# A hybrid decoder layer on 8 cores: mixer phase first, channel mixer in 1024-token tiles, probabilities as the stationary operand

## The chip, the cores and the metric

The kernel runs on the 8 cores of one Trainium2 chip. Each core computes one of the 8 sequences of the batch, with no traffic between cores. The metric is the device time in microseconds of the slowest core; lower is better. TensorE is PE in the profile, with its weight loads on a row of their own (PEld); VectorE is DVE, ScalarE is ACT, GpSimd is POOL, SyncE is SP. Every DMA is issued from the queue of an engine: in this kernel weights from POOL's, all else from SP's.

## What is computed

Per sequence of 2048 tokens and 2048 channels, one layer (the reference, cut):

```python
a = rms_norm(h, norm1_g)
q, k, v, u, sv, gates = split(a @ w_in)      # 1024 each, gates 4096
# A: 8 heads, each with two 64-wide q/k pairs and one 128-wide v
q = apply_rope(rms_norm(q)); k = apply_rope(rms_norm(k))
p = softmax(causal(q k^T / 8))               # two maps per head
o = (p[0] - lam * p[1]) @ v
o = rms_norm(o, subln_g) * 0.8
att_branch = o @ w_att_out
# B: gelu(u) * (causal 128x128 mix per group of layer_norm(gelu(sv)) + b)
sgu_branch = spatial_gating(gelu(u), gelu(sv)) @ w_sgu_out
g_att, g_sgu = split(sigmoid(gates + b_gate))
h = h + (g_att * att_branch + g_sgu * sgu_branch) @ w_out
# channel mixer
c = rms_norm(h, norm2_g)
up = causal_dwconv(c @ w_up, width 3)        # 2 * 5632
h = h + (gelu(up[:5632]) * up[5632:]) @ w_down
```

## The kernel before, in words

The program is written as one list of operations; `Sched.add` records each with the buffers that it reads and writes, and each engine runs its own operations in the order of that list, waiting on semaphores for earlier writers and readers. A read of a PSUM bank counts as a write of it. There is no scheduler: the order of the text is the order of every engine.

The outer loop takes four tiles of 512 tokens, and each tile runs the whole layer. `norm_to_T` (L331 to L350) squares and sums each of four 128-token chunks on ACT, gets the reciprocal root by Ln and Exp on ACT, scales on DVE (L339), transposes 16 blocks on PE (L346) and copies them out on DVE (L350). Then come q and k (L414, with two helper matmuls per head, L378 and L380), v (L432), u (L453) and sv (L469), v and sv in matmuls of 256 columns.

Attention runs head by head over blocks of 128 keys. Per block: two score matmuls with the keys stationary (L588, L591; 512 query columns, fewer on the diagonal), two Exp on ACT (L598, L600), a mask on the diagonal (L604), and one block later four matmuls, V or a matrix of ones stationary and the probabilities moving (L616, L619), into banks 4 to 7. The ones give the softmax sums. Then the spatial mix (L645, L650, L653), the gates and the two branch projections (L668, with the tanh of L680 and the merge of L689 to L695), and the output projection (L702, added to x in `hh`, which stays in SBUF). A second `norm_to_T` feeds the channel mixer: three groups of up to 16 hidden chunks, each up projection with convolution (L724 to L755) followed by its down projection (L768), added to `hh` (L782). The last group stores the result to `out` (L786, L779). The x loads of the next tile (L365) write `hh`, so they wait for those stores.

Weights pass through a ring of four slots of 1 MB (bf16; the source is fp32 in HBM, and the DMA of POOL's queue converts). A slot is reloaded when its last matmul has been issued (`wrel`, L262). The whole set of weights is read once per tile, four times in all.

## Time and profile before

| | |
|---|---|
| median of 3 runs | 4181.89 us (4176.98 to 4624.0) |
| profiled execution | 4176.65 us, its slowest core's span 4175.1 us |
| spans of the 8 cores | 4168.3 to 4175.1 us |
| PE busy, PEld, DVE, ACT, POOL | 90%, 46%, 42%, 30%, 7% of the span |
| DMA, POOL's queue | 494.96 MB written, 69.0% of the 16 DMA engines |
| DMA, SP's queue | 37.39 MB, 2.9% |

A matmul's end is modelled, so neighbours overlap in the busy figures; the pace of a stretch is read from starts. A DMA's bytes are those written; a weight of 1 MB in bf16 was 2 MB in HBM.

### The profile page before, as it was taken

Reading aid. Unit: us, or ns where it says so; the run is one execution under the profiler, and the core shown is the slowest. Engines: PE = TensorE matmul, PEld = TensorE weight load, DVE = VectorE, ACT = ScalarE, POOL = GpSimd, SP = SyncE. Lnnn points to the kernel's source line nnn. Section 1 sums busy time; section 2 is a strip of 40 time slices with the busy share of each in tenths; the row PEclk is TensorE's granted clock in tenths of the full one; section 3 lists DMA queues with packets and bytes.
Section 4 is the critical chain, followed back from the end, with each engine's and each line's share of the span. In section 5 each row is a group of like instructions: output and inputs, shape, how many; then the busy total and the mean of one; then the engine's idle time right before and its main releaser. Section 6 shows DMA issues by size and latency. Waiting matters only on the chain.

```text
span 4175.1 us, 56541 instructions; the slowest of 8 cores (4168.3 to 4175.1 us)
## 1 busy us (share of the span) xinstructions
PE 3774.7 (90%) x19565; PEld 1932.4 (46%) x19880; DVE 1735.9 (42%) x3544; ACT 1255.4 (30%) x2297; POOL 271.6 (7%) x516
## 2 busy tenths in 40 slices
PE   5969989995988989999598898999959989989999
PEld 2634644442553464444254346444425534554444
DVE  4251264642524137455342412645524122245545
ACT  3361031211465113112137611212214683121211
POOL 0001000000000100000000010000000000100000
PEclk9979999998999999999799999999979999999999
DMA  7809979989642878898772188789887305968887
GB/s 152 140 14 152 161 116 153 153 153 188 112 81 45 153 136 142 152 159 144 167 142 41 31 152 152 124 153 157 147 171 132 61 1 101 154 123 157 148 155 162
DMA packets 87398, 535.99 MB, mean 128 GB/s; under 512 B 9680, under 2 KB 9936, under 8 KB 29776
## 3 DMA queue, kind: packets, MB, share of 16 engines
q0 software_dynamic: 73728, 494.96, 69.0%
q1 hardware_dynamic: 13392, 37.39, 2.9%
q8 instruction: 166, 2.72, 0.3%
q14 instruction: 112, 0.92, 0.1%
HBM read 1010.46 MB, written 16.78 MB: 246 GB/s over the span
## 4 chain that ended last, share of the span: by engine, by line
PE 87%; DMA 5%; ACT 3%; DVE 3%; issue 2%; DVEq 0%; ACTq 0%; SPq 0%; POOLq 0%
PE ps L724 29%; PE ps L668 16%; PE ps L768 13%; PE ps L414 5%; PE ps L702 5%; PE ps L616 3%; PE ps L469 3%; PE ps L432 3%; PE ps L453 3%; PE ps L619 3%; DMA out<-sb_hh 3%; DMA sb_hh<-x 2%; PE ps L346 1%; PE ps L588 1%; PE ps L591 1%
## 5 line engine op out<-in xcount | busy, mean ns | idle before, releaser
L724 PE MATMUL ps<-sb_ar,sb_wr 128*128 128x512 bf16 x5516 | 1214.0, 380 | 6.8 <-issue 0.7
L724 PEld LDWEIGHTS ps<-sb_ar,sb_wr 128*128 128x128 bf16 x5632 | 552.0, 98 | 666.6 <-issue 5.4
L668 PE MATMUL ps<-sb_ar,sb_wr 128*128 128x512 bf16 x3008 | 670.3, 383 | 29.8 <-DVE sb_ar L653 17.4
L733 ACT ACTIVATE sb_tf<-ps,sb_pp 128x512 f32<-128x512 f32 x352 | 273.7, 778 | 1333.6 <-PE ps L724 1333.6
L768 PE MATMUL ps<-sb_wr,sb_ar 128*128 128x512 bf16 x2760 | 607.4, 379 | 6.5 <-DMA sb_wr<-w_down 3.5
L668 PEld LDWEIGHTS ps<-sb_ar,sb_wr 128*128 128x128 bf16 x3072 | 302.5, 99 | 396.5 <-issue 42.0
L768 PEld LDWEIGHTS ps<-sb_wr,sb_ar 128*128 128x128 bf16 x2816 | 275.2, 98 | 336.7 <-issue 5.4
L736 DVE SCALAR_TENSOR_TENSOR sb_tf<-ps,sb_pp,sb_tf 128x511 f32<-128x511 f32 x352 | 263.8, 749 | 253.9 <-ACT sb_tf L733 253.9
L782 DVE TENSOR_TENSOR sb_hh<-ps,sb_hh 128x512 f32<-128x512 f32 x176 | 121.7, 692 | 404.5 <-PE ps L768 404.5
L616 PE MATMUL ps<-sb_tb,sb_vv 128*128 128x512 bf16 (+3 forms) x627 | 220.2, 357 | 71.0 <-ACT sb_tb L598 25.7
L739 DVE SCALAR_TENSOR_TENSOR sb_tf<-ps,sb_pp,sb_tf 128x510 f32<-128x510 f32 x352 | 263.3, 748 | 38.8 <-DVE sb_tf L736 2.8
L346 PE MATMUL ps<-sb_cm,sb_ar 128*128 128x128 bf16 x512 | 59.7, 309 | 221.1 <-DVE sb_ar L339 221.1
L680 ACT ACTIVATE sb_tf<-ps,sb_hb 128x512 f32<-128x512 f32 x128 | 88.0, 687 | 517.1 <-PE ps L668 478.3
L414 PE MATMUL ps<-sb_ar,sb_wr 128*128 128x512 bf16 x1004 | 232.3, 384 | 1.7 <-DVE sb_ar L350 0.4
L619 PE MATMUL ps<-sb_tb,sb_cm 128*128 128x512 bf16 (+3 forms) x628 | 220.9, 357 | 12.1 <-ACT sb_tf L534 7.9
L702 PE MATMUL ps<-sb_wr,sb_ar 128*128 128x256 bf16 x2048 | 225.0, 273 | 1.9 <-DVE sb_ar L695 1.9
L689 DVE SCALAR_TENSOR_TENSOR sb_tf<-sb_tf,ps 128x512 f32<-128x512 f32 x64 | 43.7, 684 | 417.9 <-PE ps L668 417.9
L702 PEld LDWEIGHTS ps<-sb_wr,sb_ar 128*128 128x128 bf16 x2048 | 200.1, 98 | 27.0 <-issue 2.9
L331 ACT ACTIVATE sb_ar<-sb_hh 128x2048 bf16<-128x2048 f32 x32 | 60.8, 1899 | 481.9 <-PE ps L702 249.6
L262 POOL DMA_DIRECT2D sb_wr<-w_in x144 | 76.4, 531 | 1687.6 <-PE ps L564 567.7
L598 ACT ACTIVATE sb_tb<-ps 128x512 bf16<-128x512 f32 (+1 forms) x320 | 171.0, 534 | 44.4 <-PE ps L588 31.7
L262 POOL DMA_DIRECT2D sb_wr<-w_up x176 | 93.3, 530 | 1207.6 <-PE ps L724 892.0
(117 smaller groups left out, 3212.6 us busy)
## 6 DMA issues: line engine op xcount, KB each, us to landing
sb_wr<-w_up POOLq DMA_DIRECT2D x176, 1024.0 KB, 10.4
sb_wr<-w_in POOLq DMA_DIRECT2D x144, 1024.0 KB, 9.0
sb_wr<-w_down POOLq DMA_DIRECT2D x80, 1024.0 KB, 10.8
sb_wr<-w_out POOLq DMA_DIRECT2D x32, 1024.0 KB, 13.3
sb_hh<-x SPq DMA_DIRECT2D x16, 1024.0 KB, 12.7
sb_wr<-w_att_out POOLq DMA_DIRECT2D x32, 512.0 KB, 9.5
sb_wr<-w_sgu_out POOLq DMA_DIRECT2D x32, 512.0 KB, 8.6
out<-sb_hh SPq DMA_DIRECT2D x48, 256.0 KB, 26.7
```

The lines of the kernel that those rows point to most:

```text
L262: S.add("pool", lambda e, dst=dst, src=src: e.dma_start(out=dst, in_=src), writes=[("w", slot)], dma_key=("w", slot))
L414: S.add("pe", lambda e, bz=bz, kc=kc, wv=wv, half=half: e.matmul(ps[:, bz, :], lhsT=wv[:, kc, half * 128:(half + 1) * 128], rhs=ar[:, kc, ...
L598: S.add("act", lambda e, sb0=sb0, p0=p0, c0=c0: e.activation(out=tb[:, p0, c0:512], in_=ps[:, sb0, c0:512], func=AF.Exp), reads=[PS(sb0)], ...
L616: S.add("pe", lambda e, bo=bo, pq=pq, vsl=vsl: e.matmul(ps[:, bo, c0:512], lhsT=vsl, rhs=tb[:, pq, c0:512], start=(j == 0), stop=(j == nj ...
L619: S.add("pe", lambda e, bsum=bsum, pq=pq: e.matmul(ps[:, bsum, c0:512], lhsT=cm[:, ONES, :], rhs=tb[:, pq, c0:512], start=(j == 0), stop=( ...
L668: S.add("pe", lambda e, bk=bk, kc=kc, wv=wv, half=half, kd=kd, src0=src0: e.matmul(ps[:, bk, :], lhsT=wv[:, kc, half * 128:(half + 1) * 12 ...
L702: S.add("pe", lambda e, bk=bk, kc=kc, wv=wv, c=c: e.matmul(ps[:, bk, 0:256], lhsT=ar[:, 32 + kc, c * 128:(c + 1) * 128], rhs=wv[:, kc, :], ...
L724: S.add("pe", lambda e, bk=bk, kc=kc, wv=wv, half=half: e.matmul(ps[:, bk, :], lhsT=wv[:, kc, half * 128:(half + 1) * 128], rhs=ar[:, kc, ...
L733: S.add("act", lambda e, bk=bk, t0=t0, w2=w2, cb_=cb_: e.activation(out=tf[:, t0, :], in_=ps[:, bk, :], func=AF.Identity, scale=w2, bias=cb_),
L736: S.add("dve", lambda e, bk=bk, t0=t0, w1=w1: e.scalar_tensor_tensor(out=tf[:, t0, 1:512], in0=ps[:, bk, 0:511], scalar=w1, in1=tf[:, t0, ...
L739: S.add("dve", lambda e, bk=bk, t0=t0, w0=w0: e.scalar_tensor_tensor(out=tf[:, t0, 2:512], in0=ps[:, bk, 0:510], scalar=w0, in1=tf[:, t0, ...
L768: S.add("pe", lambda e, bk=banks[c], k=k, kl=kl, wv=wv, c=c, nch=nch: e.matmul(ps[:, bk, :], lhsT=ar[:, 16 + kl, c * 128:(c + 1) * 128], r ...
```

## The change

The layer is split into two phases. The mixer phase runs over the four tiles of 512 tokens and stores h to a buffer `h_s` in HBM; the channel mixer then runs over two tiles of 1024 tokens. One large buffer `big` and a scratch buffer `scr` hold what had tensors of their own, with keys per 128 or 512 elements.

- **Norms.** The sum of squares stays on ACT. The reciprocal root becomes a power of -0.5, a GpSimd operation (`rsq`) on POOL's queue, between two DVE operations. The first norm of tiles 1 to 3, and the second norm of the first 1024 tokens, run as generators (`side_norm1`, `side_norm2_first`) during the gate and output projections, their transposes in banks 6 and 7. The second norm of the last 1024 tokens runs in the first down projection (`norm2_next`).
- **Attention.** The probabilities are stationary, per block and component four 128x128 pieces, and V with a column of ones moves (129 columns). The accumulators of all query chunks and both components share banks 4, 5 and 6. One Exp covers both components. The normalisation runs on DVE (`fin_a` to `fin_c`), with four transposes per head at the end (`job_oT`).
- **Filling.** Matmuls of the sgu gates, the sgu projection and the spatial mix are cut into jobs that all use bank 7, and `fill` issues them between the steps of attention by a budget of nanoseconds; MM = 216 stands for a matmul.
- **Residuals.** `wo` loads x again in pieces of 128x512, adds, and stores to `h_s`; `down` loads pieces of `h_s`, adds, and stores to `out`.
- **Channel mixer.** Each weight slot serves two 512-column halves; convolution and gelu work on 1024 columns over two banks. `down` sums all 44 chunks in the eight banks before one addition.
- v, sv, the output projection and the branch projections use 512-column matmuls or slots of 8 x 512. Constants load from ACT's queue.

The core of the diff:

```diff
-        kT = sb("kT", [128, 8, SEQ], BF16)
-        hh = sb("hh", [128, 4, D], F32)
+        big = sb("big", [128, BIG], BF16)
+        scr = sb("scr", [128, 14336], BF16)
+        stg = sb("stg", [128, 2, D], BF16)
...
-        for _ in range(ntiles):
-            plan_tile()
+        for ti in range(NTILE):
...
+        for t2 in range(2):
+            for pr in range(22):
+                wplan(f"upg{pr}", wu_d[pr, 0], 16, 256)
+                wplan(f"upv{pr}", wu_d[22 + pr, 0], 16, 256)
...
+        def rsq(out, in_, n, reads, writes):
+            tt(out, in_, sc[:, SC_NH:SC_NH + 1].to_broadcast([128, n]) if n > 1 else col(sc, SC_NH), ALU.pow, reads + ["sc_nh"], writes, eng="pool")
...
+        def norm_rows(xap, xk, sl, k):
+            junk = stg[:, sl, :]
+            act(junk, xap, AF.Square, xk, [("stg", sl), ("st", k)], accum_out=col(stt, k))
+            tsc(col(stt, k + 8), col(stt, k), 1.0 / D, EPS, ALU.mult, ALU.add, [("st", k)], [("st", k + 8)])
+            rsq(col(stt, k + 8), col(stt, k + 8), 1, [("st", k + 8)], [("st", k + 8)])
+            tsc(stg[:, sl, :], xap, col(stt, k + 8), None, ALU.mult, None, xk + [("st", k + 8)], [("stg", sl)])
...
+        FB = 7
...
+        def job_gs(n_, j, ti):
...
+            for kc in range(16):
+                a, ak = aT(kc, 0, 512)
+                mm(ps[:, FB, :], wv[:, kc, half * 128:(half + 1) * 128], a, kc == 0, kc == 15, [wk] + ak, FB)
+                if kc < 15:
+                    yield MM
+            d, dk = ts(j)
+            act(d, ps[:, FB, :], AF.Tanh, [PS(FB), "hb"], dk, scale=0.5, bias=col(hb, 16 + j))
...
+            total = 16 * 16 * MM + 16 * 8 * MM + 8 * 230
+            edge = 12 * MM
+            per = (total - 8 * edge) / (8.0 * nj)
...
+                    p_, pk = npt()
+                    act(p_[:, :, c0:512], ps[:, 2 * pr:2 * pr + 2, c0:512], AF.Exp, [PS(2 * pr), PS(2 * pr + 1)], pk)
...
+                    if j == 1:
+                        fill(edge)
+                    if pav is not None:
+                        pav()
...
+                    def av(j=j, r=r, p_=p_, pk=pk, hd=hd):
+                        v_, vk = vv(j, hd, 129)
+                        for comp in range(2):
+                            for c in range(max(r, 0), 4):
+                                b, o = acc(comp, c)
+                                mm(ps[:, b, o:o + 129], p_[:, comp, c * 128:(c + 1) * 128], v_, j == 0 and (c == 0 or (c == 3 and comp == 0)),
+                                   j == nj - 1, vk + pk, b, skip_group_check=True)
+                    pav = av
+                    fill(per)
...
+            def evac(cb, c, bk):
+                t, tk_, i = pieces.pop((cb, c))
+                stto(t, ps[:, bk, :], 0.5, t, ALU.mult, ALU.add, [PS(bk)] + tk_, tk_)
+                rows = slice(tok0 + c * 128, tok0 + (c + 1) * 128)
+                dma(h_d[rows, cb * 512:(cb + 1) * 512], t, tk_, [("hd", 4 * ti + c)], ("h", i))
+                load()
...
+        def norm2_next():
+            for c in range(8):
+                xt, xk = xs2()
+                dma(xt, h_d[T2 + c * 128:T2 + (c + 1) * 128, :], [("hd", 8 + c)], xk, ("x", 2))
+                norm_rows(xt, xk, c % 2, c)
+                yield None
+                for G in range(0, 4, 2):
+                    yield (c, G)
...
+                        if s_ == 5:
+                            t, tk_ = rs2(c)
...
+                            tt(t, ps[:, c, :], t, ALU.add, [PS(c)] + tk_, tk_)
+                            dma(out_d[rows, cb * 512:(cb + 1) * 512], t, tk_, [("o", c, cb)], ("o", c))
+                            if c >= 2:
+                                side_T(c - 2)
...
+        up(0)
+        down(0, norm2_next())
+        up(1)
+        down(1, iter(()))
```

Three places show what this does to the order of the engines. In every new row the line is that of a helper, so the tiles tell what it is.

PE at the start of the first tile's attention, before: scores (kT), then four matmuls of V and ones with the probabilities (tb) moving.

```order
L469 MATMUL ps<-sb_wr,sb_ar 128x256 x256
L588 MATMUL ps<-sb_ar,sb_kT 128x512
L591 MATMUL ps<-sb_ar,sb_kT 128x512
L588 MATMUL ps<-sb_ar,sb_kT 128x384
L591 MATMUL ps<-sb_ar,sb_kT 128x384
L616 MATMUL ps<-sb_tb,sb_vv 128x512
L619 MATMUL ps<-sb_tb,sb_cm 128x512
```

The same place in the changed kernel: rows with big and scr are scores (128x512, 384, 256) or P times V (128x129), rows with wr are gate matmuls of the filling jobs, and wTm is the spatial mix.

```order
L343 MATMUL ps<-sb_wr,sb_big 128x512 x128
L343 MATMUL ps<-sb_scr,sb_big 128x512 x2
L343 MATMUL ps<-sb_big,sb_wr 128x512 x10
L343 MATMUL ps<-sb_scr,sb_big 128x384 x2
L343 MATMUL ps<-sb_big,sb_wr 128x512 x6
L343 MATMUL ps<-sb_wTm,sb_big 128x128 x4
L343 MATMUL ps<-sb_big,sb_wr 128x512 x5
L343 MATMUL ps<-sb_big,sb_scr 128x129 x8
L343 MATMUL ps<-sb_big,sb_wr 128x512 x9
L343 MATMUL ps<-sb_scr,sb_big 128x256 x2
```

The first job (10 + 6 matmuls), the spatial mix and the next job stand one right behind the other, all in bank 7.

PE in the first down projection of the changed kernel (big and wr are down matmuls; cm and stg are the transposes of the second norm):

```order
L343 MATMUL ps<-sb_big,sb_wr 128x512 x2816
L343 MATMUL ps<-sb_wr,sb_big 128x512 x332
L975 MATMUL ps<-sb_cm,sb_stg 128x128 x8
L343 MATMUL ps<-sb_wr,sb_big 128x512 x4
L975 MATMUL ps<-sb_cm,sb_stg 128x128 x8
L343 MATMUL ps<-sb_wr,sb_big 128x512 x4
```

And SP's queue at the same place (the eight residual pieces, three stores, then the first 128x2048 chunk of h for the norm):

```order
L361 DMA sb_scr<-h_s 128x512 x8
L361 DMA out<-sb_scr 128x512 x3
L361 DMA sb_scr<-h_s 128x2048
L361 DMA out<-sb_scr 128x512 x2
L361 DMA sb_scr<-h_s 128x2048
```

Each chunk's load stands in SP's queue behind the store that belongs to the down chunk just before its transposes.

## Rows read from the trace of the kernel before

**Rows 1.** Page: the span, busy time of the engines, granted clock in 40 slices

```profile
span 4175.1 us, 56541 instructions; the slowest of 8 cores (4168.3 to 4175.1 us)
...
PE 3774.7 (90%) x19565; PEld 1932.4 (46%) x19880; DVE 1735.9 (42%) x3544; ACT 1255.4 (30%) x2297; POOL 271.6 (7%) x516
...
PEclk9979999998999999999799999999979999999999
```

**Rows 2.** Windows: start, first attention, second norm, boundary of tiles 0 and 1, a dense stretch

```profile
core 4: us, PE busy (x) PEld busy (x) DVE busy (x) ACT busy (x) POOL busy (x), PEclk, DMA share, GB/s
0.00:59.50 59.50, 8.46 (x72) 7.47 (x74) 21.30 (x51) 11.37 (x18) 2.46 (x8) 1.00 0.78 179
...
205.50:290.80 85.30, 48.61 (x228) 24.15 (x233) 50.34 (x139) 60.09 (x133) 0.53 (x1) 0.73 0.04 7
...
520.00:541.00 21.00, 7.69 (x65) 6.86 (x67) 14.20 (x20) 10.46 (x17) 0.53 (x1) 0.61 0.41 68
...
997.70:1055.10 57.40, 7.46 (x64) 6.72 (x66) 14.31 (x20) 10.95 (x17) 0.53 (x1) 0.54 0.77 186
...
1560.00:2003.00 443.00, 440.72 (x2008) 200.59 (x2048) 241.41 (x527) 92.62 (x133) 33.92 (x64) 1.00 0.85 148
```

**Rows 3.** Timeline of PE (start, duration, instruction, idle before it) at that boundary

```profile
987.16 10.52 PE L768 MATMUL ps<-sb_wr,sb_ar 128*128 128x512 bf16 x47 [0.59 <-DMA sb_wr<-w_down]
1039.35 1.87 PE L346 MATMUL ps<-sb_cm,sb_ar 128*128 128x128 bf16 x16 [41.67 <-DVE sb_ar L339]
```

**Rows 4.** Chain of waits: two neighbouring runs of 49 matmuls in the up projection

```profile
551.93 10.74 PE ps L724 x49
562.73 10.74 PE ps L724 x49
```

**Rows 5.** Timeline of PE: runs with 256 and with 128 columns

```profile
177.39 28.11 PE L469 MATMUL ps<-sb_wr,sb_ar 128*128 128x256 bf16 x256
...
3458.96 2.01 PE L645 MATMUL ps<-sb_wTm,sb_ar 128*128 128x128 bf16 x32
```

**Rows 6.** Timeline of all engines: one bank from PE to ACT and back

```profile
235.69 0.38 PE L564 MATMUL ps<-sb_osqb,sb_cm 128*128 128x512 bf16 x1
...
236.16 0.69 ACT L566 ACTIVATE sb_tf<-ps,sb_sc 128x512 f32<-128x512 f32 x1 [0.62 <-PE ps L564]
...
236.99 0.32 PE L588 MATMUL ps<-sb_ar,sb_kT 128*128 128x384 bf16 x1 [0.28 <-ACT sb_tf L566]
```

**Rows 7.** Groups by line (count, busy us, mean ns, idle us before)

```profile
L331 ACT ACTIVATE sb_ar<-sb_hh 128x2048 bf16<-128x2048 f32 x32 | 60.8, 1899 | 481.9 <-PE ps L702 249.6 <-DMA sb_hh<-x 232.2 <-issue 0.2
...
L339 DVE TENSOR_SCALAR sb_ar<-sb_hh,sb_stt 128x2048 bf16<-128x2048 f32 x32 | 40.9, 1278 | 133.2 <-ACT sb_stt L335 133.2
...
L650 DVE SCALAR_TENSOR_TENSOR ps<-ps,sb_pp,sb_b 128x512 f32<-128x512 f32 x32 | 24.0, 751 | 0.0
...
L653 DVE TENSOR_TENSOR sb_ar<-ps,sb_ar 128x512 bf16<-128x512 f32 x32 | 22.1, 692 | 3.3
...
L680 ACT ACT_TABLE_LOAD x8 | 10.3, 1283 | 31.2 <-PE ps L668 27.4 <-DVE sb_ar L570 3.7
```

**Rows 8.** Page: DMA queues (packets, MB, share of 16 engines)

```profile
q0 software_dynamic: 73728, 494.96, 69.0%
q1 hardware_dynamic: 13392, 37.39, 2.9%
```

**Rows 9.** Windows: the output projection, and x loading alone

```profile
462.00:520.00 58.00, 57.36 (x518) 50.41 (x516) 16.27 (x37) 0.50 (x1) 4.24 (x8) 1.00 1.01 168
...
36.00:48.00 12.00, 1.87 (x16) 1.63 (x16) 4.71 (x6) 7.33 (x12) 0.00 (x0) 1.00 0.97 326
```

**Rows 10.** DMA queues while output stores compete with weights, us 964 to 996

```profile
q0 software_dynamic: 722, 4.09, 86.6%
q1 hardware_dynamic: 676, 1.24, 11.3%
```

**Rows 11.** Tile hh: time from issue to landing of its DMAs

```profile
DMA to landing us min/median/max: 8.4/21.4/44.5
```

More of the change, by code:

```diff
@@ L16 @@
 NTILE = 4
+T2 = 1024
 INC = 9216
@@ new lines, in job_sgu @@
+        def job_sgu(n_, j, ti):
+            if j % 4 == 0:
+                n_["s"] = wacq(f"sgu{j // 4}")
+            n, wk, wv = n_["s"]
+            q = j % 4
+            for kc in range(8):
+                a, ak = ug(kc)
+                mm(ps[:, FB, :], wv[:, kc, q * 128:(q + 1) * 128], a, kc == 0, kc == 7, [wk] + ak, FB)
+                if kc < 7:
+                    yield MM
+            d, dk = ts(j)
+            stto(d, d, 1.0, ps[:, FB, :], ALU.add, ALU.mult, dk + [PS(FB)], dk)
+            if q == 3:
+                wrel(n)
+            yield MM
@@ new lines, in job_oT, with acc @@
+        def job_oT(hd, ob, obk):
+            pv = ps[:, FB, :].bitcast(BF16)
+            for c in range(4):
+                S.add("pe", lambda e, c=c: e.transpose(out=pv[:, c * 128:(c + 1) * 128], in_=ob[:, c * 128:(c + 1) * 128], identity=cm[:, IDENT, :]),
+                      reads=obk + ["cm"], writes=[PS(FB)])
+            d, dk = qo(hd, 0, 512)
+            tsc(d, pv[:, 0:512], col(sc, SC_SUBG), None, ALU.mult, None, [PS(FB)] + SCALL, dk)
+            yield 4 * 60
+        def acc(comp, c):
+            b = 6 if c == 3 else 4 + comp
+            o = (comp if c == 3 else c) * 129
+            return b, o
@@ new lines, in attention @@
+                    pav = av
+                    fill(per)
+                    if fin is not None and j == 2:
+                        ob = fin_c(fin)
+                        urgent.append(job_oT(hd - 1, *ob))
+                        fin = None
+            pav()
+            fin = fin_a(7)
+            fin_b(fin)
+            fill(edge)
+            ob = fin_c(fin)
+            urgent.append(job_oT(7, *ob))
+            while urgent or jobs or fs["cur"] is not None:
+                fill(1000.0)
@@ new lines, in build @@
+        for ti in range(NTILE):
+            tok0 = ti * T
+            c_, ck = cs(0)
+            s_, sk = cs(1)
+            dma(c_, cos_d[:, tok0:tok0 + T], [], ck, "cos")
+            dma(s_, sin_d[:, tok0:tok0 + T], [], sk, "sin")
+            proj(ti)
+            attention(ti)
+            if ti < NTILE - 1:
+                side = side_norm1(ti + 1)
+                nn = 18
+            else:
+                side = side_norm2_first()
+                nn = 41
+            merge(ti, side)
+            wo(ti, [side, 0], nn)
```

1104 lines of the change are left out of this document (570 added, 534 removed).

## The prediction, made before the changed kernel ran

> **What bounds the kernel now.** I read the page first. PE is busy 90% of the span, the other engines 42% or less, and the granted clock is full nearly everywhere [rows 1]. So what counts is how many PE columns there are, and where PE stands still.
>
> The windows say where. The dense stretch has PE busy 440.72 of 443.00 us at a clock of 1.00, the level of 2.4 GHz, with DMA at 0.85. At the start, the second norm and the tile boundary PE works 8 us of 59.5, 21 and 57.4 us [rows 2]. At the boundary PE stands idle 41.67 us in one piece before its first transpose [rows 3], as x can't be loaded before the last stores have left `hh`.
>
> The pace of PE I take from starts. Fifty matmuls of 512 columns take 10.80 us, 0.216 each [rows 4]; 256 of 256 columns take 28.11 us, 0.110 each; 32 of 128 columns, each with fresh weights, 2.01 us, 0.058 each [rows 5]. Columns / 2.4 GHz + 2.5 ns fits all three. Over the order of the old build (19,880 matmuls) that makes 3,689 us of the span of 4,175; the other 486 are idle time or slow clock. The start has 51 of it, three boundaries 50 each, four second norms 17 each, first attention (85.3 us for 30 us of columns) 56 [rows 2], and the three later ones most of the rest.
>
> **The change, part by part.** I sum up the new kernel from zero: its matmuls at that pace, and each place where PE must stand.
>
> *Matmuls.* The new order has 18,824: 15,680 of 512 columns, 2,176 of 129, 840 of 128, 64 each of 256 and 384. That is 3,571 us, 118 less, nearly all from P times V: a full block had 4 x 0.216 = 0.86 us and has 8 x 0.058 = 0.46. No row has a matmul of 129 columns; the bounds are 0.058 [rows 5] and the 0.110 of the next form, +113 us. I take 0.058, since those 32 also changed weights every time. Wider matmuls for v, sv and output change nothing, as 256 columns cost half of 512 [rows 4, 5].
>
> *Start, 48 us.* Of 59.5 us, 51 were idle. Two x chunks now go ahead of the constants, so the first norm begins earlier, but chunks 3 and 4 wait for their buffers. Four weight slots still compete. I take 3 us less: between 40 and 55. Eight constant matmuls now stand before the projections.
>
> *Boundaries.* The norms of tiles 1 to 3 hide beside the merge and the output projection, ACT idle there and DVE with 16 of 58 us [rows 9]. The 150 and 68 us of boundaries and second norms go. What this triggers comes below, as their loads fall into the stage with DMA at 1.01.
>
> *Attention starts, 16 us.* The scores still wait for gelu, square and the masked q: 4 us per tile.
>
> *Bank 7, 225 us.* This is the largest new wait. All filling jobs accumulate in one bank, so PE can't begin the next job before ACT or DVE has emptied it, and behind that matmul stand the scores and P times V, PE being in order. The trace has this turn once: a 512-column matmul starts at 235.69, its ACT reader at 236.16, the next matmul that needed the bank at 236.99 [rows 6]. That is 1.30 us from start to start, 1.08 lost. A DVE reader takes 0.692, the same; the spatial mix has two, 0.751 + 0.692, and they lose 1.9 [rows 7]. There are 47 such turns per tile, 188 in all, and in 144 of them nothing stands between the two jobs: 54 after a gate job, 51 after an sgu job, 22 after a mix, 17 after a head's transposes (0.7). That is 58 + 54 + 42 + 12 = 166, and 22 for the 44 turns with scores or P times V between. Then queueing: tanh behind an Exp of two banks, and DVE readers behind the 13 operations of `fin_a` and `fin_b`, some 4.5 us per head. I put 37. The low end is 166, the high end 280.
>
> *Clock in attention, 15 us.* The first attention was granted 0.73 with PE busy 48.61 of 85.30 [rows 2]. The new one has about 105 us of matmuls in 155, better but not dense. Between 0 and 30.
>
> *Output projection, 117 us.* DMA share is already 1.01 at 168 GB/s written [rows 9]. To this the change adds per tile, in 55 us of matmuls: 4.2 MB of x again, 4.2 MB of h out, and about 2 MB of x for the norm. SP's queue moved 37.39 MB in 2.9% of the span, 309 GB/s [rows 8]. Work: eight slots at 6.2 us = 50, less three that the ring holds ahead = 31, and 27 + 7 for SP's queue: 65 us for 55. And it isn't shared well. With both queues full, each served about as many packets, 722 and 676, and SP's are small: it got 1.24 MB in 32 us, 39 GB/s [rows 10]. So residual pieces arrive late, their banks stay full (six of them), and PE waits until the ring is full and POOL's queue silent. I add 15: 25 us per tile, three times. The last tile loads eight chunks of h for the second norm: 31 + 27 + 27 = 85 and 12 for the queueing, 42 over. The low end is 10 in all, if the pieces slip through; the high end is the rival below.
>
> *First down projection, 112 us.* The order shows the chunk's load, its norm and its transposes with no matmul between. PE waits for: the reader of the down chunk 0.4 + 0.69 (SP's load stands behind its store), the load, 1.90 on ACT, three tiny operations, 1.28 on DVE [rows 7]. A chunk of 1.05 MB at 326 GB/s [rows 9] is 3.2 us of transfer; the shortest landing in the old trace is 8.4 [rows 11]. I take 6.5. The tiny ones have no row; between 0 and the 0.69 of a 512-column one, 0.3 each, 0.9. With semaphores 12 us, and there are eight chunks: 96 (67 to 116). Then PE restarts at 1.2 GHz, as after the gap at the boundary (clock 0.54 [rows 2]): 2 us each, 16.
>
> *Rest, 18 us.* Tail 4 as now, end of the second norm 3, ring and queue trifles 11. Up projections: weights are read twice instead of four times, DMA falls to half; DVE, 3 of 7 us per chunk, isn't late. Its saved time is worth nothing, as it lay beside PE.
>
> Sum: 3,571 + 48 + 16 + 225 + 15 + 117 + 112 + 18 = 4,122 us of span, 53 less than 4,175. The profiled execution had 4,176.65 and the median is 4,181.89, so 4,124 to 4,128 on the metric: 1.3% faster. Less than 2% either way (4,098 to 4,266) is about what this kernel's measurement can't tell from no change.
>
> **The rivals.**
> - *The new waits are light.* The pieces slip through (10 for 117), bank 7 has little queueing (180 for 225), the clock holds. 4,122 - 107 - 45 - 15 = 3,955 at the best; taking half of it, 4,040. For it: while the old kernel's stores competed with weights, PE waited 0.59 us for a weight slot [rows 3]. Against: nobody waited for those stores.
> - *SP's queue starves in the output projection.* As long as weights are backlogged SP gets 39 GB/s. Twelve slots (eight used, four ahead) keep POOL's queue busy some 90 us; in that time SP moves 4 of its 10.5 MB, the rest takes 21 us: 111 us for 55, +56, three times; the last tile's 17 MB give +80. That is 248 for 117: 4,253; with 280 for bank 7 4,308, slower by over 2%. It decides from 65 us lost per tile. Against: PE, once stopped, releases no slots, so POOL's queue falls silent by itself.
> - *Tables.* Attention now alternates Exp and tanh 64 times. If each change loads a table, 1283 ns [rows 7], there are 128 loads, 164 us of ACT: the 64 before a tanh lie in the bank turn, +82, the others partly: 4,204 to 4,286. In the old trace a load stands before tanh (8 of them), where Ln comes between. The Trainium skill, page "ScalarE: Activation LUTs", section "Table sets: the hidden batching unit", lists tanh in the set of exp. By that rule this rival has no load at all within attention; no row of the trace shows the two side by side.
>
> **Chances.** The forecast 0.53, light waits 0.28, starving queue 0.11, tables 0.04, something else slower 0.04. The light case and a third of the forecast's spread (sizes of waits +-70 us) lie under 4,098: faster 0.42. Slower by over 2%: most of the starving case, half of tables and the rest, 0.13. The remainder, 0.45, is no difference. The range 3,980 to 4,215 leaves out the best end of the light case and the worst of the two slow ones, about 0.2.
>
> **What would show it.** In the new profile: PE idle before gate, sgu and mix matmuls in attention, released by ACT or DVE, about 40 waits of 1 us per tile; output projections of 75 to 80 us with PE released by DVE readers that waited for pieces of x; eight idle times of 12 us before transposes in the first down projection, and clock at half behind them; matmuls of 129 columns at starts 0.058 apart; up projections with no idle time and DMA share near 0.45. The forecast is wrong if dense stretches lose the full clock, if the 129-column matmuls take 0.1 us, or if the waits on bank 7 are hidden by something that the order does not show.

## The result: 4.6% slower than before, where 1.3% faster was forecast

The median of the changed kernel is 4373.73 us (4362.94 to 4906.84), that of before in the same runs 4179.43. The ratio is 1.0459, with a 95% interval of 1.0431 to 1.0487. The highest of the changed kernel's times is from an execution in which four cores ran at a granted clock of 0.81; such executions are left out of every ratio here. 1% of the time before is 42 us. The forecast of 4,125 and its range up to 4,215 were missed, and slower by over 2% had been given 0.13.

The page after, of the slowest core, against [rows 1, 8]: 118 us fewer columns, and yet PE is busy a smaller share of a longer span. The granted clock shows many 8s, in the first half above all, where the old row was nearly all 9s.

```profile
span 4370.7 us, 48925 instructions; the slowest of 8 cores (4336.5 to 4370.7 us)
...
PE 3763.7 (86%) x18824; PEld 1754.1 (40%) x18824; DVE 1442.0 (33%) x2286; ACT 974.0 (22%) x1222; POOL 245.4 (6%) x416
...
PEclk9988889899898999999998999999778999999999
...
q0 software_dynamic: 49536, 356.54, 47.7%
q1 hardware_dynamic: 42624, 102.78, 7.8%
```

Where the time lies is read from windows by stage. I take core 4 (4,367.1 us), the core of the rows of before; core 3, the slowest, had a stretch at a lower clock of its own (told at the end). The columns are the stretch and its length, busy time of PE, PEld, DVE, ACT and POOL, the granted clock, the DMA share and GB/s.

```profile
0.00:56.10 56.10, 8.47 (x73) 7.31 (x73) 19.18 (x41) 9.29 (x9) 4.67 (x12) 1.00 0.83 190
56.10:203.60 147.50, 147.50 (x672) 66.19 (x672) 51.84 (x87) 57.05 (x106) 10.08 (x19) 1.00 0.77 133
203.60:434.20 230.60, 134.77 (x673) 60.94 (x674) 82.87 (x209) 35.97 (x53) 16.54 (x22) 0.84 0.33 61
434.20:622.00 187.80, 148.96 (x704) 67.84 (x702) 47.18 (x71) 18.89 (x24) 15.00 (x24) 0.89 0.90 168
...
767.30:1000.00 232.70, 159.40 (x993) 81.14 (x994) 83.14 (x209) 67.85 (x85) 16.71 (x22) 0.88 0.32 60
1000.00:1181.60 181.60, 151.66 (x704) 68.59 (x703) 47.13 (x71) 18.89 (x24) 14.96 (x24) 0.90 0.90 174
...
1326.80:1574.80 248.00, 184.81 (x1314) 100.60 (x1314) 83.23 (x209) 100.14 (x117) 16.71 (x22) 0.93 0.31 58
1574.80:1765.40 190.60, 154.98 (x729) 69.87 (x727) 49.08 (x73) 18.89 (x24) 15.06 (x24) 0.92 0.90 175
...
1910.60:2194.00 283.40, 218.45 (x1633) 118.43 (x1634) 82.89 (x206) 131.37 (x145) 16.00 (x21) 0.92 0.25 45
2194.00:2398.40 204.40, 154.54 (x769) 71.87 (x767) 63.39 (x95) 27.01 (x32) 15.39 (x28) 0.88 0.85 180
2398.40:3007.00 608.60, 608.58 (x2812) 275.59 (x2813) 288.91 (x307) 146.74 (x131) 22.70 (x43) 1.00 0.44 81
3007.00:3373.30 366.30, 251.51 (x1182) 118.15 (x1181) 48.46 (x57) 18.16 (x18) 14.01 (x26) 0.83 0.44 98
```

In order: start; projections of tile 0; its attention; its merge and output projection; attention and merge of tiles 1, 2 and 3; the first up projection; the first down projection as far as its last wait. Against the prediction's own stages:

| stage | predicted | measured | of it columns at full pace |
|---|---|---|---|
| four attentions | 846 | 995 (230.6 + 232.7 + 248.0 + 283.4) | 590 |
| four merges and output projections | 687 | 764 (187.8 + 181.6 + 190.6 + 204.4) | 577 |
| channel mixer | 1,957 | 1,969 | 1,832 |
| start | 52 | 56 | |

The predicted figures are its terms put together: 590 of columns + 16 + 225 + 15; 570 + 117; 1,832 + 112 and most of the rest; 48 and 4 of columns. The third cut of merge and output projection also holds the first 24 matmuls of the next projections, 5 us of columns; so it has 577 where the prediction had 570. The 149, 77, 12 and 4 us are nearly all of the 245 by which the span missed 4,122. The dense stages came out as predicted: 672 matmuls of 512 columns are 145.2 us at 0.216, and in the first three tiles took 145.2 to 147.5; the up projection stands nowhere, with the DMA share at 0.44.

So the question is why two stages lost so much more than predicted. PE's idle time in the four attentions is 297 us (241 predicted, starts included); the other 107 us of loss is matmuls at the lower clock (15 predicted). The second attention's largest waits, by who ended them:

```profile
PE ps L343 <- DVE sb_big L349: 20.8, 8, 5.6
PE ps L343 <- DVE sb_big L358: 15.9, 10, 5.1
PE ps L343 <- ACT sb_big L346: 12.6, 11, 1.5
PE ps L614 <- DVE sb_scr L349: 6.4, 1, 6.4
```

The last numbers are us, times and the longest. After a gate job (ACT L346) PE waits 1.1 us on average for the bank, as priced by [rows 6]. After a job that DVE empties (L358 an sgu job, L349 on big a mix), the longest waits are five times that. The last row is no wait for bank 7: it is PE before the transposes of the last head, standing until that head is normalised.

Over the four attentions the waits for bank 7, those ended by ACT L346 and DVE L349, L353 or L358 on big, add up to 243 us (85, 61, 48 and 49) in 150 waits: not far from the 225 predicted. The waits before the last head's transposes are 27 us more, the starts 15, and 12 are small ones.

Why some waits for bank 7 are so long, two timelines of the first attention tell. PE:

```profile
265.59 0.38 PE L614 MATMUL ps<-sb_cm,sb_scr 128*128 128x128 bf16 x4 [1.14 <-ACT sb_big L346]
271.62 0.58 PE L343 MATMUL ps<-sb_wTm,sb_big 128*128 128x128 bf16 x4 [5.65 <-DVE sb_big L353]
274.12 1.87 PE L343 MATMUL ps<-sb_big,sb_wr 128*128 128x512 bf16 x4 [1.91 <-DVE sb_big L349]
275.78 0.84 PE L343 MATMUL ps<-sb_scr,sb_big 128*128 128x384 bf16 x2
```

and DVE in the same microseconds:

```profile
265.18 0.17 DVE L638 RECIPROCAL sb_rr<-ps 128x3 f32<-128x3 f32 x1
...
267.47 1.72 DVE L358 SCALAR_TENSOR_TENSOR sb_scr<-ps,sb_rr,sb_scr 128x128 f32<-128x128 f32 x4
...
270.88 0.17 DVE L355 TENSOR_SCALAR sb_rr<-sb_rr 128x4 f32<-128x4 f32 x1
270.99 0.48 DVE L353 TENSOR_SCALAR sb_big<-ps,sb_sc 128x512 bf16<-128x512 bf16 x1
```

A head's four transposes are done at 266; their reader in bank 7 (L353) starts at 270.99, since `fin_a` and `fin_b` of the next head stand ahead of it in DVE's queue. PE waits 5.65 us for 0.48 us of work. And the four 512-column matmuls behind the second wait take 1.66 us from start to start, where full pace is 0.86: they run at 1.2 GHz (granted clock 0.50 from 274 to 276 us).

### The profile page after: what moved, and what is told of

Read it like the earlier page. It is cut to its first block, busy times and chain, and to the rows that moved or that the text cites. A ratio compares the mean times of both kernels' runs of the same rounds, so it can differ in the third digit from the quotient of the medians.

```text
span 4370.7 us, 48925 instructions; the slowest of 8 cores (4336.5 to 4370.7 us)
## 1 busy us (share of the span) xinstructions
PE 3763.7 (86%) x18824; PEld 1754.1 (40%) x18824; DVE 1442.0 (33%) x2286; ACT 974.0 (22%) x1222; POOL 245.4 (6%) x416
## 4 chain that ended last, share of the span: by engine, by line
PE 80%; DMA 9%; DVE 6%; issue 2%; ACT 2%; SPq 0%; DVEq 0%; POOL 0%; ACTq 0%; POOLq 0%
PE ps L343 79%; DMA h_s<-sb_scr 4%; DMA sb_scr<-x 2%; DMA sb_scr<-h_s 1%; ACT sb_scr L346 1%; DVE sb_scr L349 1%; DVE sb_scr L358 1%; DVE sb_big L358 1%; DMA sb_big<-h_s 1%; ACT sb_big L346 1%; DVE sb_big L349 1%; DVE ps L358 1%; DMA sb_pp<-pp 0%; ACT sb_stg L346 0%; DVE sb_stg L353 0%
## 5 line engine op out<-in xcount | busy, mean ns | idle before, releaser
L343 PE MATMUL ps<-sb_big,sb_wr 128*128 128x512 bf16 x10240 | 2370.7, 388 | 192.5 <-DVE sb_big L349 72.7
L343 PEld LDWEIGHTS ps<-sb_big,sb_wr 128*128 128x128 bf16 x10240 | 1002.2, 100 | 1395.6 <-issue 346.0
L343 PE MATMUL ps<-sb_wr,sb_big 128*128 128x512 bf16 x4864 | 1107.0, 389 | 30.4 <-DVE sb_scr L358 30.3
L343 PEld LDWEIGHTS ps<-sb_wr,sb_big 128*128 128x128 bf16 x4864 | 481.5, 100 | 608.3 <-issue 93.2
L358 DVE SCALAR_TENSOR_TENSOR sb_scr<-ps,sb_pp,sb_scr 128x1023 f32<-128x1023 f32 x352 | 451.4, 1282 | 572.5 <-ACT sb_scr L346 553.7
L346 ACT ACTIVATE sb_scr<-ps 128x1024 bf16<-128x1024 f32 (+1 forms) x448 | 362.8, 810 | 655.0 <-PE ps L343 642.9
L346 ACT ACTIVATE sb_scr<-ps,sb_pp 128x1024 f32<-128x1024 f32 x176 | 212.0, 1204 | 1017.2 <-PE ps L343 917.3
L349 DVE TENSOR_TENSOR sb_scr<-ps,sb_scr 128x512 f32<-128x512 f32 x64 | 44.2, 691 | 556.0 <-PE ps L343 554.9
L343 PE MATMUL ps<-sb_scr,sb_big 128*128 128x512 bf16 (+3 forms) x640 | 181.9, 368 | 14.7 <-DVE sb_scr L353 14.7
L343 PE MATMUL ps<-sb_big,sb_scr 128*128 128x129 bf16 x2176 | 183.4, 226 | 6.3 <-DVE sb_scr L349 5.4
L349 DVE TENSOR_TENSOR sb_big<-sb_scr 128x1024 bf16<-128x1024 bf16 (+1 forms) x152 | 152.2, 1001 | 50.0 <-ACT sb_scr L346 41.5
L346 ACT ACTIVATE sb_big<-ps 128x512 bf16<-128x512 f32 x80 | 47.8, 597 | 408.6 <-PE ps L343 408.5
L349 DVE TENSOR_TENSOR sb_scr<-sb_scr,sb_cm 128x256 bf16<-128x256 bf16 x128 | 37.4, 292 | 295.5 <-ACT sb_scr L346 295.4
L346 ACT ACTIVATE sb_scr<-sb_scr 128x1024 bf16<-128x1024 f32 (+1 forms) x152 | 132.2, 870 | 8.4 <-DVE sb_scr L358 2.2
L358 DVE SCALAR_TENSOR_TENSOR sb_scr<-sb_scr,ps 128x512 f32<-128x512 f32 x64 | 44.0, 688 | 250.6 <-PE ps L343 250.6
L349 DVE TENSOR_TENSOR sb_big<-ps,sb_pp 128x512 bf16<-128x512 bf16 (+1 forms) x112 | 83.6, 765 | 123.6 <-PE ps L383 107.3
L346 ACT ACTIVATE sb_scr<-ps,sb_hb 128x512 f32<-128x512 f32 x64 | 44.0, 687 | 311.4 <-PE ps L343 311.4
L358 DVE SCALAR_TENSOR_TENSOR sb_scr<-ps,sb_sc,sb_scr 128x512 f32<-128x512 f32 x128 | 95.2, 748 | 40.1 <-PE ps L343 19.2
```

What stands on the lines that cost most here:

```text
L343: S.add("pe", lambda e: e.matmul(out, lhsT=lhsT, rhs=rhs, start=start, stop=stop, **kw), reads=reads, writes=[PS(bank)])
L346: S.add("act", lambda e: e.activation(out=out, in_=in_, func=func, **kw), reads=reads, writes=writes)
L349: S.add(eng, lambda e: e.tensor_tensor(out=out, in0=in0, in1=in1, op=op), reads=reads, writes=writes)
L358: S.add("dve", lambda e: e.scalar_tensor_tensor(out=out, in0=in0, scalar=scalar, in1=in1, op0=op0, op1=op1), reads=reads, writes=writes)
```

## The experiments

Ratios are to the kernel before, with the 95% interval; the changed kernel has 1.0459.

**Three score banks, one Exp per component: the control.**

```diff
+                    sb_ = lambda i, q=2 * (hd * nj + j): (q + i) % 3
-                    act(p_[:, :, c0:512], ps[:, 2 * pr:2 * pr + 2, c0:512], AF.Exp, ...)
+                    for i in range(2):
+                        act(p_[:, i, c0:512], ps[:, sb_(i), c0:512], AF.Exp, ...)
```

> A control for the next run. The scores use three banks in turn, one bank and one Exp of 512 columns per component, where the change uses two pairs of banks and one Exp of 1024. The filling jobs keep bank 7 alone. If the loss in attention is the wait for bank 7 (theory A), this leaves it: PE idle in the four attentions stays near the 305 us measured on core 4, and the time moves by no more than the 320 extra ACT instructions and the lost slack of the fourth bank bring, -20 to +40 us. If the long Exp in front of each tanh were what the jobs wait for (rival B), shorter Exps would cut the waits behind gate jobs (0.93 us each), and the time would fall by 30 us or more.

Measured: 1.0443 [1.0416, 1.0470], no change. The attentions of core 4 took 983 us, with 294 idle. Rival B, that tanh stood behind a long Exp, falls: the Exps are half as long and nothing came back.

**Two banks for the filling jobs.** The edit above, and:

```diff
-        FB = 7
+        FBS = [7, 3]
...
+            return FBS[fbn[0] % 2]
```

Each job takes the next bank of the list.

> As the control, and the filling jobs now alternate between bank 7 and bank 3, which the scores no longer need. Theory A (one bank, one turn after another): a job's 8 to 16 matmuls (1.7 to 3.5 us) cover the turn of the bank before, so of the 305 us of idle time in attention about 166 to 200 go, and with it half of the 99 us that slow clock costs: 200 to 250 us less than the control. Theory C (the waits are the DVE queue, whose readers stand behind the 13 operations of fin_a and fin_b): both banks have their readers on the same queue, so only the short waits go, and the long ones of 5 us stay: 60 to 120 us less.

Measured: 0.9873 [0.9849, 0.9897]; 4128.77 us, where the control had 4370.42. By the ratios the second bank is worth 238 us, and it turns the loss into a gain of 1.3%. The four attentions:

```profile
202.20:361.20 159.00, 118.53 (x673) 59.69 (x674) 81.25 (x209) 37.83 (x85) 16.46 (x22) 0.91 0.50 89
...
692.90:860.40 167.50, 140.23 (x993) 78.17 (x994) 82.48 (x209) 71.89 (x149) 16.68 (x22) 0.96 0.52 86
...
1185.00:1377.80 192.80, 169.88 (x1314) 97.15 (x1314) 82.87 (x209) 106.24 (x213) 16.68 (x22) 0.98 0.39 74
...
1704.50:1932.20 227.70, 200.78 (x1634) 116.24 (x1634) 83.34 (x209) 140.20 (x277) 16.54 (x22) 0.97 0.33 59
```

They sum to 747 us, 236 less than the control; idle time fell from 294 to 118, and the waits for the bank alone from 239 to 61. The granted clock, 0.84 to 0.93 in the control, rose to 0.91 to 0.98. Besides 176 us of idle time, 60 us of slow clock went. Theory A holds, and C in its pure form (60 to 120) does not: two banks cover the queue on DVE too, as the next job, of 1.7 to 3.5 us, runs meanwhile.

**A head's transposes emptied by ACT.**

```diff
-            tsc(d, pv[:, 0:512], col(sc, SC_SUBG), None, ALU.mult, ...)
+            act(d, pv[:, 0:512], AF.Copy, [PS(FB)] + SCALL, dk)
+            tsc(d, d, col(sc, SC_SUBG), None, ALU.mult, None, dk + SCALL, dk)
```

> The change, with one edit: the bank of a head's four transposes is emptied by an ACT copy, and the scaling by DVE follows on that copy in SBUF. Bank 7 is then free after the ACT copy. Theory C: the waits of 5 to 5.7 us behind a head's transposes go (28 heads without a tail: up to 140 us if all have them, about 50 us if the first tile alone has them, since in later tiles more steps lie between), and some half clock with them: 50 to 150 us less. Theory A in its plain form (every turn costs its 0.7 to 1.1 us, the queue little) expects less than 25 us.

Measured: 1.0413 [1.0394, 1.0432], 19 us less, though this interval and that of the changed kernel just touch. On core 4 the first attention took 205.6 us for 230.6, the other three the same as before the edit. The wait that the timeline shows so plainly is one of tile 0 alone: DVE L353 on big ended 23.2 us of waits in its attention and 3.3 in the next. In later tiles more steps lie between. My theory C was too large for this place.

**No normalisation.** `fin_a`, `fin_b` and `fin_c` are replaced by three copies and one scaling.

```diff
-            S.add("dve", lambda e: e.reciprocal(out=r[:, 4:7], in_=bB[:, :, 128]), ...)
...
+            S.add("dve", lambda e: e.tensor_copy(out=f0[:, 0:384]..., in_=bA[:, :, 0:128]), ...)
+            S.add("dve", lambda e: e.tensor_copy(out=f0[:, 384:512], in_=bC[:, 0, 0:128]), ...)
+            S.add("dve", lambda e: e.tensor_copy(out=r[:, 4:7], in_=bB[:, :, 128]), ...)
...
+            tsc(ob, f0, 0.001, None, ALU.mult, None, f0k, obk)
```

> The normalisation of each head is left out: instead of the 13 operations of fin_a and fin_b (some 5.6 us in one piece on VectorE) three short copies free banks 4, 5 and 6, and one scaling makes the input of the transposes. The filling jobs keep bank 7 alone. If the burst in VectorE's queue makes the long waits of the filling jobs (theory C), 28 bursts cost 3 to 5 us each with the half clock behind them: 80 to 150 us less. If the plain turn of one bank is the loss (theory A), little goes but the waits at the four tails: 10 to 50 us less.

Measured: 1.0140 [1.0115, 1.0164], 133 us less. The first two attentions (core 2, mean clock 0.957):

```profile
201.00:379.60 178.60, 121.52 (x673) 57.16 (x674) 51.12 (x129) 35.98 (x53) 8.34 (x14) 0.94 0.41 73
...
708.60:914.40 205.80, 151.92 (x994) 78.79 (x994) 51.66 (x129) 67.91 (x85) 8.44 (x14) 0.94 0.38 64
```

With 223.7 and 267.6 for the others that is 876 us, idle 203, where the changed kernel has 297. So about 95 us of its idle time come from the burst on DVE (31 us of work per tile, 83 to 51), with 25 us of slow clock. The waits for bank 7 fell from 243 to 173 us: 70 us were queueing, behind sgu and mix jobs as well as transposes, and the longest wait there is now 2.1 us. The prediction had 37 for all queueing, and 188 for the turns themselves. The waits before the last head's transposes fell from 27 to 6 us; the prediction had no term for them. A second bank removes more, 176 us of idle time.

**The weaving undone.** Only a head's four transposes stay between the steps of attention; the other jobs follow it, in five banks.

```diff
-                    if j == 1:
-                        fill(edge)
...
+            FBS[:] = [7, 0, 1, 2, 3]
             fill(edge)
```

> The weaving undone: no filling between the steps of attention; the gate, mix and projection jobs follow after the last head, in five banks in turn. If weaving in one bank is what costs (theory A), the jobs run dense (about 75 us per tile) and attention alone goes at the pace of its Exps, some 1.1 us per block of keys, 320 blocks, where PE has 0.9 us of work: about 70 us idle and 30 at heads' ends, against 305 now, so 100 to 200 us less than the change. If the filling does its work (theory D: without it PE stands between scores and P times V, and the granted clock falls to the lower level for whole heads), it is as slow as the change or slower by up to 150 us.

Measured: 1.0228 [1.0203, 1.0252], 97 us less than with weaving. On core 4 the attentions took 96.4, 119.2, 157.9 and 196.4 us and the jobs behind them 331, together 901 for 997 in the same cuts. The first attention, and its jobs:

```profile
201.50:297.90 96.40, 46.53 (x274) 27.70 (x275) 61.05 (x177) 25.03 (x38) 9.63 (x10) 0.59 0.07 13
297.90:380.40 82.50, 82.50 (x402) 38.25 (x400) 22.34 (x32) 10.31 (x15) 5.87 (x11) 0.98 0.78 137
```

Weaving into one bank was worse than no weaving; weaving into two is better than none by 148 us (1.0228 to 0.9873). Theory D is not empty: without the filling the first attention had a clock of 0.59.

**Residual pieces not loaded.** This leaves the residual x out.

```diff
-                    dma(t, x_d[rows, cb * 512:(cb + 1) * 512], [], tk_, ...)
...
-                stto(t, ps[:, bk, :], 0.5, t, ALU.mult, ALU.add, [PS(bk)] + tk_, tk_)
+                tsc(t, ps[:, bk, :], 0.5, None, ALU.mult, None, [PS(bk)], tk_)
```

> The 64 loads of residual pieces of x are left out, and x is not added: this leaves out the residual of the mixer phase, 16.8 MB of loads. PE stands idle 145 us in the four stretches of merge and output projection, in waits of 9 to 20 us, behind DVE readers that waited for a piece of x (55 us of DVE's waiting in the first such stretch). Theory P (the pieces are the late ones): the 95 us of the first three stretches go, and most of the half clock behind them: 100 to 140 us less than the change. Rival W (the stage lacks DMA in total, and the chunks of the side norm come as late): the waits move to the transposes of the norm, 20 to 60 us less. The last tile, whose waits are for chunks of h, keeps its 50 us in both.

Measured: 1.0208 [1.0186, 1.0230], 105 us less. For merge, output projection and the next projections of tile 0, the changed kernel needed 333.1 us and this one 304.5:

```profile
432.10:736.60 304.50, 289.61 (x1349) 132.60 (x1374) 96.19 (x142) 76.97 (x130) 24.43 (x43) 0.99 0.89 163
```

Over three tiles the idle time there fell from 104 to 33 us. What waited in the changed kernel, in the window 434.2:622 (engine, line, us, times, longest):

```profile
DVE sb_scr L358 <- DMA sb_scr<-x: 55.4, 9, 15.8
...
PE ps L383 <- DVE sb_big L349: 23.4, 2, 20.4
```

DVE stands 55 us for pieces of x. The reader of the side norm's transposes stands behind it, and PE 20.4 us behind that reader. Nothing in PE's row names the piece: the DVE queue has to be followed one step further.

**The pieces asked for earlier.** Ten slots, five loads before the merge and five at the start of the output projection.

```diff
-            for _ in range(4):
+            for _ in range(5):
                 load()
+            yield                 # merge
+            for _ in range(5):
+                load()
```

> The same loads, earlier: ten slots for the residual pieces instead of five shared ones, five loaded before the merge and five at the start of the output projection, where the change loads four at that start. Nothing less is transferred. If the pieces are late because they are asked for late (theory P1), the first ten are there in time and six are left for the crowded stretch: 60 to 100 us less. If SP's queue gets too small a share as long as weights are in POOL's (theory P2, the rival of the prediction), the later six pieces and the norm's chunks wait as before: 0 to 40 us less.

Measured: 1.0488 [1.0460, 1.0515], no gain. In this run cosine and sine rows came late in turn, with 12 us of waits in the projections of tile 1. Even with these counted as an effect of the edit, 60 to 100 us are out of reach, so P1 falls: being late in asking was not the cause.

**Half of each output weight.** This leaves out half of w_out.

```diff
-                wplan(f"wo{b}", wt_d[4 + b // 2, b % 2], 8, 512)
+                wplan(f"wo{b}", wt_d[4 + b // 2, b % 2][:, 0:2048], 4, 512)
```

> Each weight of the output projection is loaded by half, and the matmuls of its other half read the first half again: this leaves out half of w_out, 4 of the 8 MB per tile. The loads of x and the stores of h stay as the change has them. If the stage lacks DMA in total (theory P3: 8 MB of weights at 164 GB/s and 8.4 MB of pieces and stores plus the norm's chunks at 243 GB/s, the rates of the two queues in this stage, are some 90 us of transfers for 55 us of matmuls), halving the weights frees 25 us per tile, and the pieces come in time: 70 to 110 us less, as without the pieces. If the pieces are late because SP's queue works in order, each load behind a store that waits for VectorE (rival), they stay late: less than 30 us.

Measured: 1.0301 [1.0276, 1.0326], 66 us less, a little under the 70 to 110 that P3 expected and well over its rival's 30. Idle time in the three stretches fell from 104 to 60 us. So it is the total of the transfers that the stage is short for. The queues of the changed kernel from 520 to 622 us (packets, MB, share of 16 engines) give the price:

```profile
q0 software_dynamic: 1282, 9.29, 55.4%
q1 hardware_dynamic: 4068, 8.17, 33.0%
```

Weights moved at 9.29 MB / (0.554 x 102 us) = 164 GB/s, SP's queue at 8.17 / (0.330 x 102) = 243. The prediction priced SP's queue at 309 [rows 8]. From these two rates I estimate a tile at 8.4 MB of weights / 164 = 51 us and 10.5 MB / 243 = 43 us: 94 us of transfers for 55 of matmuls, 39 too many. SP's queue wasn't starved: it moved 80 GB/s over the window, where the rival had 39, and took 37% of the time in use. One packet of weights takes 0.705 us of an engine, one of SP's 0.132, so if both queues always had packets waiting and took strict turns, it would get 16%. The Trainium skill, page "DMA: Bandwidth & Descriptors", section "Queues, rings and completion order", says that a DMA engine takes turns between the queues it has work for, one packet each. That agrees with [rows 10], 722 packets to 676. Here there were 3.2 packets of SP's to one of weights; by that rule POOL's queue had nothing to send for part of the time.

**The second norm spread over the down projection.** Two chunks per column block are loaded and normed in its first steps, their transposes follow in its last.

```diff
+                    if side and s_ in (0, 2):
+                        norm2_load(2 * cb + s_ // 2)
...
-                            if c >= 2:
-                                side_T(c - 2)
+                            if side and 2 <= c < 6:
+                                side_T(c - 2, 2 * cb + (c - 2) // 2, 2 * (c % 2))
```

> The second norm in the first down projection is spread: two chunks of h per column block are loaded and normed during the first steps of that block, and their transposes follow in its last step, where the change does load, norm and transposes of a chunk with no matmul between. Theory N (each chunk's chain stands in PE's way, eight times 11 to 18 us): the 115 us of idle time go and some half clock, 95 to 125 us less than the change. Rival: DVE and ACT readers or the weights at a DMA share near 0.9 are late instead, and less than 60 us come back.

Measured: 1.0118 [1.0100, 1.0136], 143 us less, more than expected. On core 4 everything after the last attention took 2,041.8 us for 2,173.1:

```profile
2178.30:4220.10 2041.80, 1975.17 (x9159) 905.60 (x9342) 746.30 (x897) 339.52 (x313) 93.25 (x168) 0.99 0.53 106
```

111 us of that is idle time (165 to 53), 20 is clock.

**Everything together,** with the next chunk's norm issued ahead of the transposes in the last mixer tile.

```diff
+            rows_(0)
             for c in range(8):
-                xt, xk = xs(c % 2)
-                norm_rows(xt, xk, c % 2, c)
...
                     norm_T(c % 2, G, 6 + G % 2, dst, dk, PP_N2G)
                     yield 0
+                    if G == 0 and c + 1 < 8:
+                        rows_(c + 1)
```

> All at once: two banks for the filling jobs (242 us less than its control), a head's transposes emptied by ACT (13 to 17 us less alone), the residual pieces earlier, the second norm spread, and in the last mixer tile the norm of the next chunk issued ahead of the transposes of the one before. If each place costs by itself, the sum of the single results: 4,374 - 242 - 15 - about 80 - about 105 - 20 = 3,910 us, 6.5% faster than before. If one stage's gain is given back in the next (transfers that meet in the output projection as the attention gets shorter), 3,960 to 4,050.

Measured: 0.9581 [0.9562, 0.9600], 4004.51 us. The single results would give 1.0459 - 0.0570 - 0.0046 + 0.0029 - 0.0341 = 0.9531; 21 us were given back or never there. This is the second case of the expectation, whose 3,910 still had 80 us for the earlier pieces, which their own run did not show. The norm ahead brought nothing visible: the last output projection still had waits of 27 and 15 us. In the projections of tile 1 PE stood 15 us, for cosine and sine rows.

**Cosine and sine rows before attention.**

```diff
             proj(ti)
+            if ti < NTILE - 1:
+                dma(c_, cos_d[:, tok0 + T:tok0 + 2 * T], [], ck, "cos")
+                dma(s_, sin_d[:, tok0 + T:tok0 + 2 * T], [], sk, "sin")
```

> The combined kernel of the last group, with the loads of the cosine and sine rows of the next tile issued before attention, where DMA is busy a third of the time; in the combined kernel they landed late, behind the stores of h, and TensorE stood 15 us in the first projection of tile 1. Expected: 10 to 30 us less than the combined kernel, 3,975 to 3,995. If that wait only hid a lack of transfers that then shows at a weight: no difference.

Measured: 0.9549 [0.9530, 0.9567], 3993.70 us: 13 us less, the small end of the gain expected, and the two intervals overlap a little. On core 4 merge, output projection and next projections of tile 0 went from 344.0 to 325.8 us. DVE no longer waits for cosine or sine there, but PE still stands 12 us at the first projections, now behind DVE readers that wait 16 us for pieces of x: part of the wait had only hidden the next one.

**`fin_b` one step later.**

```diff
                         fin = fin_a(hd - 1)
-                        fin_b(fin)
+                    elif j == 1 and fin is not None:
+                        fin_b(fin)
```

> The last combined kernel (bank pair for the filling jobs, ACT reader, pieces and rows of cosine earlier, spread norm), and the four operations of fin_b one step of attention later than the nine of fin_a, so that VectorE has no burst of 13. With two banks the queue behind the burst is left in the waits of 3 to 4 us of the first attention (40 us idle in all there, 34 in the combined kernel). If these come from the length of the burst: 10 to 35 us less than the combined kernel, about 3,970. If the nine operations that free the accumulators are what counts, or the two banks already hide the burst: no difference, 3,985 to 4,000.

Measured: 0.9460 [0.9434, 0.9487], 3959.27 us: 5.4% faster than before, and 37 us less than without this edit, just over the 10 to 35 expected. Attention, once 230.6 and 232.7 us in the first two tiles:

```profile
202.50:340.70 138.20, 111.24 (x660) 57.68 (x674) 79.79 (x209) 41.46 (x92) 16.54 (x22) 0.96 0.59 108
...
662.10:823.80 161.70, 137.53 (x975) 77.09 (x994) 80.97 (x209) 75.57 (x156) 16.63 (x22) 0.98 0.51 92
```

Splitting a burst of 13 operations into 9 and 4 is worth 30 us in attention even with two banks (715 for 744 us over the four).

## Why the prediction failed, step by step

- **What bounds the kernel, matmuls:** right. 18,824 matmuls ran, and the unknown price of 129 columns is 0.056: the eight that start at 2041.24 end where the next row starts, 0.45 us later.

```profile
2041.24 0.62 PE L343 MATMUL ps<-sb_big,sb_scr 128*128 128x129 bf16 x8
2041.69 0.59 PE L343 MATMUL ps<-sb_big,sb_wr 128*128 128x512 bf16 x2
```

- **Start, boundaries:** the start took 4 us more than predicted, and the norms of tiles 1 to 3 did vanish as such.
- **Bank 7, 225 us: nearly right, and 243 measured.** The turns cost 173 us without the burst (188 forecast), the queueing 70 (37 forecast). The prediction knew the burst (4.5 us per head, 144 for 32 heads) and charged a quarter of it where about half came. The last head of each tile has no such place in the sum: PE waited 27 us before its transposes, and that term was put at nothing. With the clock behind the waits, one bank instead of two costs 238 us.
- **Clock in attention, 15 us: the step that failed most.** It was 107, where the high end was 30. I had read the level of the first attention before (0.73 [rows 2]), and argued from a better busy share that the new one would lose little. The 150 waits cut PE's work into many short runs, and removing waits gave clock back with them: 236 us came back for 176 of idle time with two banks, about 120 for 95 without the burst, 131 for 111 in the down projection, 86 for 71 without the pieces. An idle microsecond in this kernel costs 1.2 to 1.3. The prediction charged 1.0 nearly everywhere.
- **Output projection, 117 us: failed as to size.** 187 measured (764 less 577), 154 idle and the rest clock. The mechanism named was the right one: late pieces, DVE readers, full banks. The step that failed is the sum of the transfers, 65 us per tile: it had SP's queue at 309 GB/s, which moved 243, and three slots of lead from the ring. With 243 and no lead my estimate above is 94; that the lead was gone I take from the DMA share of 0.90 over merge and output projection together, and no run tested it. The pieces alone were worth 105. The forecast's 25 us lost per tile were 43 (46, 40 and 43 over columns), and its 42 for the last tile 58. The rival of the starving queue is half right: the stage cost 70 us more than forecast, but it never reached 65 per tile, and SP's queue wasn't starved. (Its 4 MB in 90 us at 39 GB/s are 3.5; that adds 2 us to its 111.)
- **First down projection, 112 us:** eight waits as named, and longer than 12 each:

```profile
L975 PE MATMUL ps<-sb_cm,sb_stg 128*128 128x128 bf16 x128 | 16.6, 309 | 114.8 <-DVE sb_stg L353 114.8
```

  That is 14.4 us each. Most of the difference is the chunk's load, priced at 6.5 us: from its issue to the start of ACT's square the eight took 5.3 to 11.7 us, 8.4 on average, and longest for the first of a column block. One of them:

```profile
3209.15 0.33 SPq L361 DMA_DIRECT2D sb_scr<-h_s  x1
3220.07 1.91 ACT L346 ACTIVATE sb_stg<-sb_scr 128x2048 bf16<-128x2048 f32 x1 [90.25 <-DMA sb_scr<-h_s]
3224.58 1.01 PE L975 MATMUL ps<-sb_cm,sb_stg 128*128 128x128 bf16 x8 [16.79 <-DVE sb_stg L353]
```

  With the clock behind them the chain cost 143 by its removal.
- **Tables:** no cost. Each attention has one table load, at its start, and 16 tanh between its Exps; the whole kernel has 13. The second attention, by ACT:

```profile
L346 ACT ACTIVATE sb_scr<-ps 128x1024 bf16<-128x1024 f32 (+1 forms) x64 | 55.2, 863 | 133.4 <-PE ps L343 132.8 <-DVE sb_scr L349 0.6
L346 ACT ACTIVATE sb_big<-ps,sb_hb 128x512 f32<-128x512 f32 x16 | 10.9, 684 | 17.6 <-PE ps L343 17.6
L346 ACT ACT_TABLE_LOAD x1 | 1.3, 1283 | 3.1 <-PE ps L343 3.1
```

  The Trainium skill, page "ScalarE: Activation LUTs", section "Table sets: the hidden batching unit", lists tanh in the set of exp; by that rule no load stands between the two, and the trace agrees.
- **Range and chances:** of the 245 us missed, 92 are the clock in attention, 70 the output projections, 27 the last heads' normalisation, 18 bank 7 and 12 the channel mixer. All these errors went one way, and slow matmuls behind waits are in several of them (107 us in attention, 33 in the output projections, about 18 in the down projection, 31 forecast in all). The range took the terms' bounds as if they were independent; the starving queue with the high end of bank 7 made 4,308, and even that was overshot.

Still open: what is left of the 187 us in the output projections beside the residual pieces, in the last tile above all. Moving its transfers into attention, where the DMA share is 0.3 to 0.6, needs space in SBUF and was not tried.

## What to carry to other kernels

Give work that is woven in to fill gaps two accumulator banks of its own: here, with one, jobs ended in 150 waits, each as long as the bank's turn and the queue of the engine that empties it. Price a wait by everything ahead of its releaser in that engine's queue, and look for bursts there; cutting one into two gave 37 us here. And charge idle time of TensorE with the slow matmuls behind it: in this kernel 1.2 to 1.3 us per us.

## What the runs showed that I had not expected

The power operation on POOL takes 1,031 ns for 128x4 elements and 559 for 128x1; the prediction had put each tiny operation at 0.3 us. It lies in each of the eight chains of the down projection.

```profile
L349 POOL TENSOR_TENSOR sb_rr<-sb_rr,sb_sc 128x4 f32<-128x4 f32 x32 | 33.0, 1031 | 552.7 <-DVE sb_rr L355 552.7
...
L349 POOL TENSOR_TENSOR sb_stt<-sb_stt,sb_sc 128x1 f32<-128x1 f32 x32 | 17.9, 559 | 345.6 <-DVE sb_stt L355 345.6
```

Core 3, the slowest of the profiled execution, had a granted clock of 0.81 from 440 to 600 us, PE busy 157.35 of 160 us for 639 matmuls:

```profile
440.00:600.00 160.00, 157.35 (x639) 66.85 (x637) 41.26 (x61) 18.10 (x23) 13.50 (x23) 0.81 0.88 161
```

Core 4 had 0.94 there, with PE busy 134.60 for 647. Core 3 ended only 3.6 us later: in this stage the slower matmuls took the place of waits for transfers, which is one more sign that DMA bounds it. Core 2 shows the same stretch (0.81, PE busy 155.22 us), cores 0 and 1 don't (0.92 and 0.91); why the clock was lower there stays open.
